# Splitting the streamed weights four chunks ahead in place of three, in a ring of five slots

## The chip, the core and the metric

The kernel runs on one core of one Trainium2 chip. The metric is device time in microseconds (us) of one execution. Engines are called by their names here: TensorE (PE) multiplies, VectorE (DVE) and ScalarE (ACT) do elementwise work, GpSimd (POOL) does some elementwise work and issues transfers, SyncE (SP) issues transfers alone.

## What is computed

Two transformer-like layers run one after the other on x, 256 tokens of width 1024, all in float32:

- First layer: a norm, one projection to queries, keys, values and gates, a differential attention (8 heads) and a chunk attention (8 heads), two branch projections weighed by gates, an output projection; then a norm and a product-key retrieval of experts ("peer"): top-16 of top-16 candidates per head, and for all 16384 experts `hid = gelu(u . x)` times a gate that is zero for those that were not picked, and a sum with the value rows v.
- Second layer: a feed-forward part (`silu(gate) * up`, width 2816), a mixer of a linear recurrence and a sliding-window attention, a second feed-forward part, each with norms before and after.

```
xn   = rmsnorm(h, norm1_w);  proj = xn @ w_in
h    = h + (g_d*(o_d @ w_branch_diff) + g_c*(o_c @ w_branch_chunk)) @ w_out
h    = h + peer(rmsnorm(h, norm2_w), ...)
x    = x + 0.5*rms_norm(swiglu(rms_norm(x)))
x    = x + rms_norm(hybrid_mixer(rms_norm(x)))
x    = x + 0.5*rms_norm(swiglu(rms_norm(x)))
```

## The kernel before

**The stream of weights.** All weights lie in DRAM as 244 chunks of 128 x 2048 float32 (1 MB each) in the order of their use: `qkd` 8, `vd` 4, `vc` 2, `qkc` 4, `gate` 8, `bd` 4, `bc` 2, `out` 4, `wq` 4, `pu` 64 (hidden units of the experts), `pv` 64 (their values), `gu1` 22, `dn1` 11, `in2` 7, `wo` 4, `gu2` 22, `dn2` 11. Every float32 product is made of three matmuls on two parts: for a weight w, `wh` is w rounded to the matmul's short form, and `wl = w - wh`; likewise `xh` and `xl`. `three` (L1917 to L1919) issues high x high, high x low, low x high.

**The ring.** `raw`, `wh` and `wl` have `RING = 5` slots each; chunk c uses slot c % 5. `raw` and `wl` share one memory (L101 to L105): the low part is written over the raw chunk, so a slot can be filled again only when TensorE has finished the chunk in it. Four engines pass a chunk on:

1. SyncE (L401) waits for `c_done`, which TensorE raises at the end of each chunk, and issues the transfer of chunk c+5 into the slot of chunk c. This we call the refill.
2. ScalarE, `split(c)` (L557 to L561): waits for the landing (`raw_in[slot]`) and casts raw to `wh`, one instruction of 128 x 2048.
3. VectorE, `low(c, slot)` (L967 to L970): waits for that cast (`w_high`) and subtracts, one instruction of 128 x 2048 (L969).
4. TensorE waits for `w_low` and runs the chunk: 48 matmuls of 256 columns, or 24 of 512.

```
def ahead(c):
    if c + AHEAD < NCH:
        split(c + AHEAD)
```

**What sets the order.** Each engine has one program, written by hand, and works through it in order. `ahead(c)` stands in the programs of ScalarE and VectorE at the places that belong to TensorE's chunk c, between the other work of that chunk, and splits the chunk `AHEAD` later. `ahead_in(i, c)` (L568, L976) is the same inside the loops over the expert values. Two short runs at the start split the first chunks.

**The stages in which other work stands beside the splits.**

- Attention of the first layer, 24 steps n (two steps to a chunk of `qkc` and `gate`). TensorE's step: transpose the weights of step n (L2042), scores of step n+2 (L2032), one half of a chunk (`gates_beside(n + 1)`, 24 matmuls), values of step n (`output`, L2056). In an even step that half ends a chunk and raises `c_done`. ScalarE's step: scale the output of step n-1 (L691), copy the transposed weights of step n to memory (L682), exponentials of step n+2 (L673), and in even steps `ahead(CH["qkc"] + n // 2 + 1)`. TensorE's values of step n wait for the copy of step n.
- Branch projections `bd`, `bc` (VectorE L1334, L1349 to L1355): VectorE takes each finished unit out of the two banks of `ub`, and TensorE may begin the next but one only then.
- Experts, hidden part (`pu`): TensorE one chunk a step, ScalarE gelu (L766). From hidden step 34 to 57 a step also spreads the gates of one or two groups of 8 tokens (1, 1, 2 in turn): VectorE makes the one-hot rows of a group (L1462, L1467, L1471: `one1`, `one2`, `g2`), TensorE multiplies them (L2161), ScalarE copies them out (L785), and every sixth step GpSimd stores 4 MB of gates (L479). VectorE's step: one-hot rows of step n, then `ahead` of step n.
- Experts, value part (`pv`): ScalarE casts the activations (L804), VectorE subtracts (L1489), GpSimd multiplies by the gate (L499) and issues two loads of 256 KB a chunk.
- Between the parts: the sum of a stage in `acc` is squared on ScalarE (L599), and VectorE computes the norm's root and the diagonal `dg` with which TensorE transposes the next input.

Of the kernel before, what the change touches and what calls it, by code (L numbers as in the profile page):

```python
# [40 lines left out]

CW = 2048
RING = 5
AHEAD = 3
_sizes = [("qkd", 8), ("vd", 4), ("vc", 2), ("qkc", 4), ("gate", 8), ("bd", 4), ("bc", 2), ("out", 4),
          ("wq", 4), ("pu", 64), ("pv", 64), ("gu1", 22), ("dn1", 11), ("in2", 7), ("wo", 4),
          ("gu2", 22), ("dn2", 11)]
# [42 lines left out]
def build_program(nc, A, out):  # L90
    ctx = ExitStack()
    with ctx:
# [463 lines left out]
        def _(act):  # L556
            def split(c):  # L557

                slot = c % RING
                act.wait_ge(raw_in[slot], c // RING * 16 + 16)  # L560
                act.copy(wh[:, slot, :], raw[:, slot, :]).then_inc(w_high, 1)  # L561
# [6 lines that stand above are left out]
            def ahead_in(i, c):  # L568

                c += AHEAD  # L570
                slot = c % RING
# [23 lines left out]
            def square(src, scratch, col, scale=1.0):  # L595

                if nsq[0]:
                    act.wait_ge(sq_ok, nsq[0])
                act.activation(scratch[:, 0:src.shape[1]], src, ACT.Square, scale=scale,  # L599
                               accum_out=ssq[:, col:col + 1]).then_inc(sq_ok, 1)  # L600
                nsq[0] += 1
# [25 lines left out]
            def resid_of(tt):  # L627
                return resid[:, tt, :]
# [19 lines left out]
            split(1)  # L648
            act.wait_ge(x_in[1], 16)
            square(resid_of(1), junk, 1)  # L650
            split(2)

            for j in range(8):
                ahead(j)
# [303 lines left out]
        def _(v):  # L958
# [8 lines left out]
            def low(c, slot):  # L967
                v.wait_ge(w_high, c + 1)
                v.tensor_tensor(wl[:, slot, :], raw[:, slot, :], wh[:, slot, :].bitcast(F32),  # L969
                                ALU.subtract).then_inc(w_low, 1)  # L970

            def ahead(c):
                if c + AHEAD < NCH:
                    low(c + AHEAD, (c + AHEAD) % RING)

            def ahead_in(i, c):  # L976

                low(i * VBODY + (c + AHEAD), (c + AHEAD) % RING)

# [231 lines left out]
                v.wait_ge(c_done, i * 4 + (j + 1))  # L1211
                scaled(qkT[:, bass.ds(i * 8 + 2 * j, 2), :], j % 2 if (i, j) != (0, 2) else None).then_inc(u_free, 1)

            low(AHEAD - 1, AHEAD - 1)
            ahead(0)
            scale_row()
            for j in range(3):
# [1203 lines left out]
```

## Time and profile before

| | |
|---|---|
| median of 3 runs | 1504.12 us (1503.8 to 1507.4) |
| the profiled execution, time | 1504.91 us |
| the profiled execution, span | 1503.4 us |
| TensorE busy | 1484.8 us (99%), weight loads 1372.2 us |
| VectorE busy | 1067.2 us (71%) |
| ScalarE busy | 729.6 us (49%) |
| GpSimd busy | 306.4 us (20%) |
| DMA | 329.76 MB, 219 GB/s over the span |
| mean granted TensorE clock | 0.999 |

The span is what the profile's rows lie in; the device time of the same execution is 1.5 us longer. An engine's share is a mean over stages with different limits; TensorE's 99% is nearly the same in all of them.

### The profile page before, as it was taken

To read this page: it belongs to the slowest core of one execution; us is meant where nothing else is said; L and a number is where in the kernel's file an instruction comes from. 1 tells how busy PE (TensorE), PEld (TensorE's weight loads), DVE (VectorE), ACT (ScalarE), POOL (GpSimd) and SP (SyncE) were. 2 spreads that over 40 slices of the span, in tenths; PEclk is the share of its full clock that TensorE was granted. 3 is DMA by queue.
4 is the path that set the end of the run, shared out by engine and by line. 5 is a ranking of instruction groups with operands and counts; after the bars stand their busy time and mean duration, and the time that the engine had idled before them with its cause. 6 is when DMAs were issued, how large, how long until landed. Compare 5 with 4: busy or idle time off the path is not lost.

```text
span 1503.4 us, 26972 instructions
## 1 busy us (share of the span) xinstructions
PE 1484.8 (99%) x10794; PEld 1372.2 (91%) x10794; DVE 1067.2 (71%) x1583; ACT 729.6 (49%) x853; POOL 306.4 (20%) x306
## 2 busy tenths in 40 slices
PE   8999999999999999999999999999999999999998
PEld 8989998999999999998888888888999898899986
DVE  5667676699999898946555555566877476787753
ACT  5366653544454454544444444445444458644441
POOL 2000000000110111125666677650000010000000
PEclk9999999999999999999999999999999999999999
DMA  8644354576666678888888788775555543455552
GB/s 305 204 157 141 122 172 173 191 245 242 234 226 214 214 253 278 286 304 312 288 288 288 288 292 292 284 272 182 197 197 196 196 162 113 154 170 196 182 187 80
DMA packets 56697, 329.76 MB, mean 219 GB/s; under 512 B 7536, under 2 KB 7584, under 8 KB 25232
## 3 DMA queue, kind: packets, MB, share of 16 engines
q1 hardware_dynamic: 36288, 259.01, 50.4%
q0 software_dynamic: 20304, 69.21, 12.6%
q8 instruction: 82, 1.34, 0.4%
q14 instruction: 23, 0.19, 0.0%
HBM read 294.64 MB, written 33.55 MB: 218 GB/s over the span
## 4 chain that ended last, share of the span: by engine, by line
PE 94%; DVE 3%; ACT 2%; issue 0%; DMA 0%; DVEq 0%; ACTq 0%
PE ub L1917 17%; PE ub L1918 17%; PE ub L1919 17%; PE acc L1919 11%; PE acc L1917 11%; PE acc L1918 11%; PE acc L2161 3%; PE acc L2032 1%; PE mb L2056 1%; PE mb L1919 1%; PE mb L1918 1%; PE mb L1917 1%; DVE wl L969 1%; PE mb L2042 0%; ACT junk_again L599 0%
## 5 line engine op out<-in xcount | busy, mean ns | idle before, releaser
L969 DVE TENSOR_TENSOR wl<-raw,wh 128x2048 fp32r<-128x2048 f32 x244 | 561.1, 2303 | 201.5 <-ACT wh L561 137.3
L1917 PE MATMUL ub<-xh,wh 128*128 128x256 f32 x2168 | 610.9, 282 | 0.8 <-DVE wl L1195 0.8
L1919 PE MATMUL ub<-xh,wl 128*128 128x256 f32 x2168 | 603.2, 278 | 0.0
L1918 PE MATMUL ub<-xl,wh 128*128 128x256 f32 x2168 | 603.2, 278 | 0.0
L1917 PEld LDWEIGHTS ub<-xh,wh 128*128 128x128 f32 x2168 | 408.1, 188 | 8.9 <-issue 6.1
L1918 PEld LDWEIGHTS ub<-xl,wh 128*128 128x128 f32 x2168 | 409.6, 189 | 0.1
L1919 PEld LDWEIGHTS ub<-xh,wl 128*128 128x128 f32 x2168 | 409.4, 189 | 0.0
L561 ACT CAST wh<-raw 128x2048 fp32r<-128x2048 f32 x184 | 350.6, 1907 | 118.6 <-DMA raw<-in_wstream 118.5
L1917 PE MATMUL acc<-wh,ah 128*128 128x512 f32 x512 | 199.4, 389 | 1.1 <-issue 1.1
L1919 PE MATMUL acc<-wh,al 128*128 128x512 f32 x512 | 199.2, 389 | 0.0
L1918 PE MATMUL acc<-wl,ah 128*128 128x512 f32 x512 | 199.2, 389 | 0.0
L499 POOL TENSOR_TENSOR hid<-hid,gl_in 128x512 f32<-128x512 f32 x64 | 157.9, 2469 | 16.7 <-DMA gl_in<-gates 15.8
L804 ACT CAST ah<-hid 128x512 fp32r<-128x512 f32 x64 | 39.9, 623 | 187.6 <-PE acc L1919 185.2
L766 ACT ACTIVATE hid<-ub 128x512 f32<-128x512 f32 x64 | 38.3, 599 | 159.5 <-PE ub L1919 158.3
L1917 PEld LDWEIGHTS acc<-wh,ah 128*128 128x128 f32 x512 | 96.1, 188 | 21.0 <-issue 1.3
L573 ACT CAST wh<-raw 128x2048 fp32r<-128x2048 f32 x60 | 114.2, 1904 | 0.8 <-DMA raw<-in_wstream 0.8
L1919 PEld LDWEIGHTS acc<-wh,al 128*128 128x128 f32 x512 | 96.1, 188 | 20.0
L1918 PEld LDWEIGHTS acc<-wl,ah 128*128 128x128 f32 x512 | 96.1, 188 | 20.0
L462 POOL DMA_DIRECT2D hidden<-hid x60 | 32.6, 544 | 366.9 <-ACT hid L766 366.9
L1489 DVE TENSOR_TENSOR al<-hid,ah 128x512 fp32r<-128x512 f32 x64 | 49.2, 768 | 81.8 <-ACT ah L804 81.8
L842 ACT ACTIVATE fs<-fg 128x256 f32<-128x256 f32 x44 | 18.4, 418 | 137.5 <-DVE fg L1085 137.5
L1919 PE MATMUL acc<-wh,fl 128*128 128x512 f32 x176 | 68.5, 389 | 0.0
(379 smaller groups left out, 1759.2 us busy)
## 6 DMA issues: line engine op xcount, KB each, us to landing
raw<-in_wstream SPq DMA_DIRECT2D x244, 1024.0 KB, 4.9
gates<-gst POOLq DMA_DIRECT2D x16, 1024.0 KB, 14.7
gl_in<-gates POOLq DMA_DIRECT2D x64, 256.0 KB, 3.7
hidden<-hid POOLq DMA_DIRECT2D x60, 256.0 KB, 4.9
hid<-hidden POOLq DMA_DIRECT2D x60, 256.0 KB, 3.6
resid<-in_x SPq DMA_DIRECT2D x2, 512.0 KB, 4.2
rb<-in_rel POOLq DMA_DIRECT2D x1, 1024.0 KB, 6.0
wb<-in_ffn_post_g POOLq DMA_DIRECT2D x2, 512.0 KB, 4.8
```

Of the source, the lines that this page charges most:

```text
L462: pool.dma_start(hidden[bass.ds(n + 4, 1)].rearrange("a p n -> p (a n)"), hid[:, k, :, :].rearrange("p a b -> p (a b)")).then_inc(spill[k] ...
L499: pool.tensor_tensor(h, h, gl_in[:, k, :].rearrange("p (g j t) -> p j g t", g=TG, j=2), ALU.mult).then_inc(hd_m, 1)
L561: act.copy(wh[:, slot, :], raw[:, slot, :]).then_inc(w_high, 1)
L573: act.copy(wh[:, slot, :], raw[:, slot, :]).then_inc(w_high, 1)
L766: act.activation(hid[:, nmod % 4, :, :].rearrange("p a b -> p (a b)"), ub[:, nmod % 2, :], ACT.Gelu).then_inc(hd_g, 1)
L804: act.copy(ah[:, nmod % 2, :, :], hid[:, nmod % 4, :, :]).then_inc(a_h, 1)
L969: v.tensor_tensor(wl[:, slot, :], raw[:, slot, :], wh[:, slot, :].bitcast(F32), ALU.subtract).then_inc(w_low, 1)
L1489: v.tensor_tensor(al[:, k % 2, :, :], hid[:, k % 4, :, :], ah[:, k % 2, :, :].bitcast(F32), ALU.subtract).then_inc(a_l, 1)
L1917: pe.matmul(dst, sh, mh, start=first, stop=False)
L1918: pe.matmul(dst, sh, ml, start=False, stop=False)
L1919: return pe.matmul(dst, sl, mh, start=False, stop=last)
L2161: last = pe.matmul(dst, g2[:, b, part, :, k], one2[:, b, k, :], start=part == 0, stop=part == 2)
```

## The change

`AHEAD` becomes 4, and the two runs at the start split one chunk more. Nothing else is changed: ring, transfers, TensorE's program and what is computed stay as they are.

```diff
 CW = 2048
 RING = 5
-AHEAD = 3
+AHEAD = RING - 1
...
             square(resid_of(1), junk, 1)
-            split(2)
+            for c in range(2, AHEAD):
+                split(c)
...
-            low(AHEAD - 1, AHEAD - 1)
+            for c in range(2, AHEAD):
+                low(c, c)
             ahead(0)
             scale_row()
```

What this does to the order. The orders of TensorE, GpSimd and SyncE are the same before and after. On VectorE the first difference is at the start, between the diagonal `dg` of the first norm and the copy `rt` of its row. Before:

```order
L1066 TENSOR_SCALAR dg<-ident,rstd 128x128
L969 TENSOR_TENSOR wl<-raw,wh 128x2048 [waits w_high] x2
L1080 COPY rt<-mb 128x256 [waits sc_ps]
L1085 TENSOR_TENSOR qkT<-ub,rt 128x512 [waits c_done,dve]
L1085 TENSOR_TENSOR qkT<-ub,rt 128x512 [waits c_done]
```

and with the change:

```order
L1067 TENSOR_SCALAR dg<-ident,rstd 128x128
L970 TENSOR_TENSOR wl<-raw,wh 128x2048 [waits w_high] x3
L1081 COPY rt<-mb 128x256 [waits sc_ps]
L1086 TENSOR_TENSOR qkT<-ub,rt 128x512 [waits c_done,dve]
L1086 TENSOR_TENSOR qkT<-ub,rt 128x512 [waits c_done]
```

One subtraction more stands ahead of the copy; from there to the last chunks each subtraction of a chunk stands where that of the chunk before it stood.

On ScalarE the kinds of instructions stand in the same order afterwards, but each cast waits for another slot. The opening and step 0 of the first attention (`p_sb` exponentials, `pT` the transposed weights, `y` the output), before:

```order
L561 CAST wh<-raw 128x2048 [waits raw_in2]
L682 COPY pT<-mb 128x128 [waits at_t]
L673 ACTIVATE p_sb,rs<-s_sb,smx 128x128 [waits at_b]
L673 ACTIVATE p_sb,rs<-s_sb,smx 128x128
L561 CAST wh<-raw 128x2048 [waits raw_in3]
L691 ACTIVATE y<-mb,rr 128x128 [waits at_o]
L682 COPY pT<-mb 128x256 [waits at_t]
```

and with the change:

```order
L561 CAST wh<-raw 128x2048 [waits raw_in3]
L683 COPY pT<-mb 128x128 [waits at_t]
L674 ACTIVATE p_sb,rs<-s_sb,smx 128x128 [waits at_b]
L674 ACTIVATE p_sb,rs<-s_sb,smx 128x128
L561 CAST wh<-raw 128x2048 [waits raw_in4]
L692 ACTIVATE y<-mb,rr 128x128 [waits at_o]
L683 COPY pT<-mb 128x256 [waits at_t]
```

The cast of step 0 moved from slot 3 to slot 4. Chunk `qkc` + 0, number 14, is in slot 4, and TensorE finishes it in the same step 0.

The first steps of the gates' part of the experts on ScalarE (`hid` gelu, `gst` the copied gates), before:

```order
L779 CAST gT<-mb 128x128
L561 CAST wh<-raw 128x2048 [waits raw_in2]
L766 ACTIVATE hid<-ub 128x512 [waits spill2,c_done]
L785 COPY gst<-acc 128x128x8 [waits g_ps]
L561 CAST wh<-raw 128x2048 [waits raw_in3]
```

and with the change:

```order
L780 CAST gT<-mb 128x128
L561 CAST wh<-raw 128x2048 [waits raw_in3]
L767 ACTIVATE hid<-ub 128x512 [waits spill2,c_done]
L786 COPY gst<-acc 128x128x8 [waits g_ps]
L561 CAST wh<-raw 128x2048 [waits raw_in4]
```

Again each cast waits for the slot that was filled one chunk later than the slot it waited for before.

## Rows read from the trace of the kernel before

**Rows 1.** The page, busy time and share of TensorE and its weight loads.

```profile
PE 1484.8 (99%) x10794; PEld 1372.2 (91%) x10794; DVE 1067.2 (71%) x1583; ACT 729.6 (49%) x853; POOL 306.4 (20%) x306
```

**Rows 2.** Waits of TensorE: us in total, times, longest.

```profile
PE mb L1823 <- DMA resid<-in_x: 4.8, 1, 4.8
...
PE acc L1917 <- DVE wl L969: 1.2, 1, 1.2
```

**Rows 3.** Timeline of SyncE's queue at 96 us: start, us, engine, line.

```profile
96.29 0.33 SPq L401 DMA_DIRECT2D raw<-in_wstream  x1
```

**Rows 4.** Landing of refills: at 96, 516 to 534, 538 to 555, 700 to 1020.

```profile
DMA to landing us min/median/max: 4.9/4.9/4.9
...
DMA to landing us min/median/max: 8.9/10.5/10.9
...
DMA to landing us min/median/max: 5.2/5.2/6.6
...
DMA to landing us min/median/max: 4.7/4.9/5.8
```

**Rows 5.** Timeline of ScalarE, attention steps 0 and 1.

```profile
94.66 1.89 ACT L561 CAST wh<-raw 128x2048 fp32r<-128x2048 f32 x1
96.46 0.36 ACT L691 ACTIVATE y<-mb,rr 128x128 f32<-128x128 f32 x1
96.72 0.35 ACT L682 COPY pT<-mb 128x256 f32<-128x256 f32 x1
```

**Rows 6.** Timeline of TensorE, values of attention steps 0, 1 and 2.

```profile
95.95 0.38 PE L2056 MATMUL mb<-vd,pT 128*128 128x128 f32 x2
...
99.96 0.61 PE L2056 MATMUL mb<-vd,pT 128*128 128x128 f32 x4
...
103.87 0.38 PE L2056 MATMUL mb<-vd,pT 128*128 128x128 f32 x2
```

**Rows 7.** Timeline of ScalarE, gates' part: gelu of two steps.

```profile
540.59 0.60 ACT L766 ACTIVATE hid<-ub 128x512 f32<-128x512 f32 x1 [2.68 <-PE ub L1919]
...
547.64 0.60 ACT L766 ACTIVATE hid<-ub 128x512 f32<-128x512 f32 x1 [2.68 <-PE ub L1919]
```

**Rows 8.** Timeline of VectorE, gates' part: first one-hot instruction of two groups.

```profile
547.21 0.68 DVE L1462 TENSOR_TENSOR one<-iota,i1T 128x1024 bf16<-128x1024 bf16 x1
...
550.72 0.69 DVE L1462 TENSOR_TENSOR one<-iota,i1T 128x1024 bf16<-128x1024 bf16 x1
```

**Rows 9.** Timeline of VectorE at places between the parts.

```profile
213.64 2.29 DVE L969 TENSOR_TENSOR wl<-raw,wh 128x2048 fp32r<-128x2048 f32 x1 [1.08 <-ACT wh L561]
215.85 0.68 DVE L1349 TENSOR_TENSOR gate<-ub,gate 128x512 f32<-128x512 f32 x1
...
239.23 1.22 DVE L1172 TENSOR_TENSOR resid<-resid,acc 128x1024 f32<-128x1024 f32 x1 [1.83 <-PE acc L1919]
...
1210.34 1.22 DVE L1113 TENSOR_TENSOR y_again<-acc,wb 128x1024 f32<-128x1024 f32 x1 [2.83 <-ACT junk_again L599]
```

**Rows 10.** Timeline of ScalarE at places between the parts.

```profile
217.99 1.91 ACT L561 CAST wh<-raw 128x2048 fp32r<-128x2048 f32 x1 [4.38 <-DMA raw<-in_wstream]
...
664.97 1.91 ACT L561 CAST wh<-raw 128x2048 fp32r<-128x2048 f32 x1 [4.87 <-DMA raw<-in_wstream]
...
1286.39 1.06 ACT L931 ACTIVATE gl<-gl 128x1024 f32<-128x1024 f32 x1
```

**Rows 11.** Timeline of ScalarE, value part: cast of the activations, two chunks.

```profile
764.26 0.62 ACT L804 CAST ah<-hid 128x512 fp32r<-128x512 f32 x1 [3.01 <-PE acc L1919]
...
769.71 0.62 ACT L804 CAST ah<-hid 128x512 fp32r<-128x512 f32 x1 [3.01 <-PE acc L1919]
```

**Rows 12.** Timeline of VectorE, value part: low part of the activations.

```profile
764.92 0.69 DVE L1489 TENSOR_TENSOR al<-hid,ah 128x512 fp32r<-128x512 f32 x1 [1.34 <-ACT ah L804]
```

**Rows 13.** Timeline of TensorE: a matmul at 9.8 us, one at 18 us.

```profile
9.80 0.41 PE L1919 MATMUL ub<-xh,wl 128*128 128x256 f32 x1
...
18.04 0.28 PE L1918 MATMUL ub<-xl,wh 128*128 128x256 f32 x1
```

## The prediction
> **What bounds the kernel now.** I read the page's busy times first: TensorE is busy 1484.8 us of 1503.4 [rows 1]. Then the waits of TensorE: the longest is 4.8 us, for x at the very start, and for the split weights (`wl`) it waits 1.2 us, once [rows 2]. So TensorE sets the time throughout, and an earlier split has next to nothing to give back: even if every wait for weights went, that is 1.2 us. The question is therefore what the change can do to TensorE's cover. For that I read the queue of SyncE with the landings, and then the timelines of ScalarE, TensorE and VectorE in each stage.
>
> **What the change really moves.** The ring decides when a chunk can be split, not `AHEAD`: chunk m can land only after TensorE has ended chunk m-5. With `AHEAD` 3 the step of chunk c asks for c+3, whose refill was issued at the end of c-2; with 4 it asks for c+4, issued at the end of c-1. The transfer starts no earlier than before; what comes earlier is the place of the waiting cast in ScalarE's program, and of the waiting subtraction in VectorE's. Everything behind them in those in-order programs now waits for a refill issued one chunk later. The price of one turn of the ring: the refill of the chunk that ended at 96.1 is issued at 96.29 [rows 3] and lands 4.9 us later [rows 4]; the cast takes 1.9 [rows 5], the subtraction 2.3 [rows 9]. So, after the end of a chunk, the cast is done at +7.0 and the subtraction at +9.3. Where a stage needs something that stands behind them sooner than that, TensorE stalls. No instruction, byte or matmul is added.
>
> **Attention of the first layer, the largest term.** In even steps TensorE ends a chunk in the half that stands before `output(n)`. ScalarE's cast of the same step now asks for the slot of just that chunk. Before, the cast of step 0 began at 94.66 without a wait, and then came the output scaling at 96.46 and the copy `pT` of step 1 at 96.72, ended at 97.07 [rows 5]; TensorE used that copy at 99.96 [rows 6]. Now the cast begins at 96.29 + 4.9 = 101.2 and the copy follows it by as much as before: it ends at 101.2 + (97.07 - 94.66) = 103.6. TensorE's values of step 1 begin there and not at 99.96: a stall of 3.65 us. Nothing recovers it, since the next chunk ends a fixed piece of TensorE's work after that point, and its refill starts the same wait again: the two-step period goes from 103.87 - 95.95 = 7.9 us [rows 6] to 11.6. There are 11 such even steps (n = 0 to 20): 11 x 3.65 = 40 us. In the last steps outputs and copies are a little longer, but so is TensorE's step; I leave 3.65. Bounds: 3.4 and 4.0 a step, 37 to 44 us.
>
> **The gates' part of the experts, the second term.** Here VectorE makes the one-hot rows of step n+1 behind the subtraction of step n. One group takes 550.72 - 547.21 = 3.5 us [rows 8]. From the issue of a refill the first group is ready after landing + 1.9 + 2.3 + 3.5 = landing + 7.7, and the second of a step 3.5 later. TensorE wants the first two steps after the chunk's end: 2 x (547.64 - 540.59) = 14.1 us [rows 7], and the second 1.6 us later (the time of one spread, a step of 7.05 less a chunk of 5.44). With a landing of 5.2 [rows 4] the first is ready at 12.9: no stall; but the second comes at 16.4 against 15.7 at the most, so steps with two groups lose about 1 to 2 us. While GpSimd's stores of the gates run, a refill lands after 8.9 to 10.9 [rows 4]; then the first group is ready at 18.6 against 14.1, a stall of 4.5 us, and the two refills behind it find the room that this stall made. Step by step through the 24 steps: 4.2 us at the entry (the one-hots stand behind the cast of chunk 37, which the last top-k steps did not need to wait for), 8 steps of two groups at 1 to 1.9, and three of the four stores at 4.7. The sum is 4.2 + 8 x 1.5 + 3 x 4.7 = 30 us. Bounds: 11 us if landings stay at 5.2 throughout (the stalled kernel has fewer refills to a store), 35 if each store costs a little more.
>
> **Places between the parts.** The same wait, met once each. Branch projections: VectorE's gating of the first `bc` unit began at 215.85, behind a subtraction from 213.64 [rows 9]. It now stands behind the subtraction of the next chunk, cast from 217.99 to 219.9 [rows 10] and subtracted until 222.2: 6.4 us later, of which 0.9 was slack, so 5.5. Output projection to `wq`: the add to the residual at 239.23 [rows 9] moves behind a subtraction that ends at 243.0, and 2.7 us of it reach the diagonal that TensorE waits for. End of the hidden part: the cast at 664.97 waited 4.9 us for its landing [rows 10]; the gelu that stands behind it now is one that TensorE needs at 664.95, so 2.5. `dn1` to `in2`: the norm at 1210.34 [rows 9] is held back 3.2 by the subtraction of the chunk whose refill is issued at 1203.8, and ScalarE's cast ahead of the next norm adds 0.4: 3.6. `wo`: the gelu at 1286.39 [rows 10] moves 2.8 back, behind a cast that must wait until 1286, and the cast ahead of the norm of the second feed-forward part adds 1.4: 4.2. Entries of the first attention and of the first feed-forward part, an estimate from the same +9.3: 3.4. Together 5.5 + 2.7 + 2.5 + 3.6 + 4.2 + 3.4 = 22. Bounds 12 and 28.
>
> **The value part.** After the end of a chunk the cast is done at +7.0, the subtraction at +9.3, and the low part of the activations (0.7, [rows 12]) at +10.0. TensorE wants it after two chunks, 2 x (769.71 - 764.26) = 10.9 [rows 11]. So 0.9 us are left a chunk, and with landings of 4.7 to 5.8 [rows 4] it just holds. But GpSimd's two loads move with the low part and will start together with the refill. I take 4 us for the first chunks, where landings are longer; the bounds are 0 and 26 (a landing that grows by 1.8 makes each of 60 chunks 0.43 longer).
>
> **Where it costs nothing.** Projections at the start, `wq`, the top-k steps (VectorE is behind there: each subtraction begins after its cast would be done also now), the bodies of both feed-forward parts, and the end (fewer splits are left): the work that hides it is TensorE's own 5.4 us chunk, since only a copy needed two chunks later stands behind the cast. In several of these stretches ScalarE already waits for landings, as at 217.99 [rows 10], and nothing moves.
>
> **The sum.** 40 + 30 + 22 + 4 = 96 us. The profiled execution took 1504.9, 0.8 above the median of 1504.1; on the median's footing I predict 1600 us.
>
> **Rivals.** (1) *The stalls also slow the matmuls.* After TensorE's idle start its matmuls of 256 columns are shown 0.41 us long, later 0.28 [rows 13], although the granted clock reads 1.00 in both stretches, so the rows do not tell this pace as the clock. If it came back after each attention stall, the 3.9 us of TensorE's work between a stall and the next end of a chunk would take up to twice that: up to 11 x 3.9 = 43 us more, about 1640. Against it: no row shows the pace fall after the short gaps of this kernel, but none of them is as long as 3.65. The Trainium skill, TensorE: Matmul & The Clock Gate, section "Why this matters for your kernels", says that idle gaps between bursts of matmuls can put TensorE back to its lower clock; by that rule the sum would be this rival's, and without it 1600. (2) *The value part stalls throughout:* the landing grows by the full 1.8 us because two loads stand in front of each refill: 1600 + 22 = 1622. For it speaks the small slack of 0.9, against it that the refills of that part landed within 5.8. (3) *Only the attention pays:* the gates' landings shorten and the places between find slack: 1504 + 40 + 11 + 12 = 1567. (4) *Not slower:* the wait changes hands. If ScalarE reached the cast of an even attention step after the refill had landed, the deeper split would hide there, TensorE's 1.2 us for `wl` would go, and the time would be 1503. It decides whether the landing (issue + 4.9) comes before ScalarE is at the cast (94.66 to 96.5); the rows put it at 101.2, so this needs ScalarE to be 5 us late, and nothing makes it so.
>
> **How the numbers follow.** Forecast 0.68, rival 1 0.12, rival 2 0.10, rival 3 0.08, rival 4 0.02. The forecast's own bounds are 37 + 11 + 12 + 0 = 60 and 44 + 35 + 28 + 26 = 133 us, that is 1564 to 1637; ends of all terms on one side at once are unlikely. I set 1570 to 1640, which takes in rivals 2 and most of 1, and leaves out about 2 in 10. A difference of 0.3% is 4.5 us, about what can be told from no change here. All cases but rival 4 are far slower: slower 0.98, same 0.015, faster 0.005.
>
> **What would show it.** TensorE's row of waits should gain two long entries: values (L2056) waiting for the copy of `pT` (L682), 11 times about 3.7 us, and spreads (L2161) waiting for the one-hot product (L1471), about a dozen times, 30 us. ScalarE's waits for landings (L561) should grow most in the attention, and the distance between refills there should be 11.6 us. The bodies of the feed-forward parts should keep 5.44 us a chunk. I am wrong if the attention's refills stay 7.9 us apart, or if the granted clock falls below 1.00 there.

## The result and the profile after

The changed kernel takes 1642.88 us (median of 4 runs, 1639.78 to 1648.12) against 1504.13: a ratio of 1.0926, 95% interval 1.0902 to 1.0949. It is slower by 139 us where 96 were forecast, and lies 3 us above the end of the range. The profiled execution has a span of 1642.7 us, 139.3 more than before.

The page of the changed kernel, busy time and the granted clock in 40 slices of 41 us (before: [rows 1], and a clock of 1.00 nearly throughout):

```profile
PE 1534.1 (93%) x10794; PEld 1400.9 (85%) x10794; DVE 1109.9 (68%) x1583; ACT 728.1 (44%) x853; POOL 263.9 (16%) x306
...
PEclk9988889999999999989999999999999999999999
```

TensorE runs the same 10794 matmuls and is busy 49.3 us longer (1534.1 against 1484.8). So about 90 of the 139 us are idle time, as the forecast had it. The rest is shown as busy: matmuls that ran slower, which the forecast had left out of its sum, and in the value part stalls too short for these rows.

Waits of TensorE in the changed kernel (before: [rows 2]; line numbers above 651 are one or two higher than before, so L2058 is the old L2056 and L2163 the old L2161):

```profile
PE mb L2058 <- ACT pT L683: 38.6, 11, 3.7
PE acc L2163 <- DVE g L1473: 23.5, 11, 4.6
PE acc L1919 <- DVE al L1491: 8.7, 19, 1.9
...
PE mb L1851 <- DVE dg L1108: 4.1, 2, 2.6
PE ub L1919 <- DVE gate L1351: 3.1, 1, 3.1
PE ub L1919 <- ACT hid L767: 2.6, 1, 2.6
PE mb L2044 <- DVE p_sb L1273: 2.3, 1, 2.3
```

The first row is the forecast's main term nearly to the digit: 11 waits of 3.5 us in the mean. The second is the gates' part with its entry, the third the value part, and the four short rows are places between the parts. In the value part the waits of the weight loads have to be read too (7.2 us for `wl`, 5.9 for `al`): TensorE is shown busy for 359.3 us there against 349.1 before, at a granted clock of 1.00 in both, so the rows of the matmuls count such short stalls as busy.

ScalarE in step 1 of the first attention, and then TensorE around the wait that it causes (before: [rows 5, 6]):

```profile
104.73 1.90 ACT L561 CAST wh<-raw 128x2048 fp32r<-128x2048 f32 x1 [7.40 <-DMA raw<-in_wstream]
106.53 0.36 ACT L692 ACTIVATE y<-mb,rr 128x128 f32<-128x128 f32 x1
106.79 0.36 ACT L683 COPY pT<-mb 128x256 f32<-128x256 f32 x1
```

```profile
103.61 0.28 PE L1921 MATMUL ub<-xh,wl 128*128 128x256 f32 x1
107.21 1.23 PE L2058 MATMUL mb<-vd,pT 128*128 128x128 f32 x4 [3.32 <-ACT pT L683]
...
109.69 0.41 PE L1920 MATMUL ub<-xl,wh 128*128 128x256 f32 x1
109.90 0.41 PE L1921 MATMUL ub<-xh,wl 128*128 128x256 f32 x1
...
113.31 0.29 PE L1919 MATMUL ub<-xh,wh 128*128 128x256 f32 x1
113.44 0.28 PE L1920 MATMUL ub<-xl,wh 128*128 128x256 f32 x1
```

ScalarE waits 7.4 us for a landing and only then makes the 0.36 us copy that TensorE needs. Behind the 3.3 us gap TensorE's matmuls of 256 columns start 0.21 us apart, until 6 us after its end, and then 0.12 apart again: the two levels, 1.2 and 2.4 GHz. The refills of the attention, 7.9 us apart before, now come 13.1 to 15.8 us apart; the forecast had 11.6. It had also named its sign of being wrong, a granted clock below 1.00 in the attention, and this came true. The stretches of the changed kernel show the clock (the columns: stretch, its length, busy time and instructions of PE, PEld, DVE, ACT and POOL, granted clock, DMA share, GB/s); they are the 6 us behind that gap, the first attention, the branch and output projections, the gates' part and the value part. Under them stands the attention before:

```profile
107.20:113.30 6.10, 6.09 (x27) 5.54 (x28) 3.64 (x9) 2.34 (x10) 0.00 (x0) 0.50 0.00 0
...
88.40:257.00 168.60, 127.71 (x833) 114.85 (x832) 75.28 (x238) 68.00 (x181) 5.09 (x6) 0.83 0.24 79
257.00:322.90 65.90, 57.97 (x395) 53.31 (x393) 38.58 (x46) 27.18 (x24) 1.63 (x2) 0.97 0.44 148
553.00:761.00 208.00, 187.60 (x1873) 184.79 (x1873) 159.90 (x118) 86.78 (x77) 26.39 (x35) 0.94 0.62 209
798.00:1168.00 370.00, 359.33 (x1542) 287.22 (x1543) 242.30 (x132) 156.05 (x131) 179.45 (x182) 1.00 0.75 267
```

```profile
88.80:188.70 99.90, 99.90 (x833) 90.92 (x833) 72.34 (x237) 67.94 (x180) 5.10 (x6) 1.00 0.40 134
```

The attention is 68.7 us longer for the same 833 matmuls: 40.9 us are idle, and the busy time grew by 27.8. Divided at the same instructions in both traces, the 139.3 us fall like this:

| part | before | after | more | forecast |
|---|---|---|---|---|
| first attention | 99.9 | 168.6 | 68.7 | 40 |
| gates' part, with its entry | 373.3 | 407.8 | 34.5 | 30 |
| value part | 349.1 | 369.5 | 20.4 | 4 |
| everything else | | | 15.7 | 22 |

(The entry of the gates' part is counted from the key scores on, 196.7 us before and 200.0 after, and the spreads themselves take 176.6 and 207.8. The row of the first attention holds that part's entry, about 3 us, which the forecast had among its 22. The last row is 20.5 us at the other places between the parts, less 4 us by which the chunks of `gu2` went through faster and 1 us in small differences; the last section comes back to these 4.)

### The profile page after: what moved, and what is told of

It reads as the page before. It is cut to its first block, busy times and chain, and to the rows that moved or that the text cites. A ratio compares the mean times of both kernels' runs of the same rounds, so it can differ in the third digit from the quotient of the medians.

```text
span 1642.7 us, 26972 instructions
## 1 busy us (share of the span) xinstructions
PE 1534.1 (93%) x10794; PEld 1400.9 (85%) x10794; DVE 1109.9 (68%) x1583; ACT 728.1 (44%) x853; POOL 263.9 (16%) x306
## 4 chain that ended last, share of the span: by engine, by line
PE 66%; DMA 16%; DVE 7%; ACT 5%; issue 5%; SPq 0%; DVEq 0%
DMA raw<-in_wstream 16%; PE ub L1919 14%; PE ub L1921 13%; PE ub L1920 13%; PE acc L1919 7%; PE acc L1921 7%; PE acc L1920 7%; ACT wh L561 2%; ACT wh L573 2%; DVE wl L970 2%; DVE g L1473 2%; PE acc L2163 1%; DVE one L1469 1%; PE mb L2058 1%; DVE al L1491 1%
## 5 line engine op out<-in xcount | busy, mean ns | idle before, releaser
L970 DVE TENSOR_TENSOR wl<-raw,wh 128x2048 fp32r<-128x2048 f32 x244 | 588.3, 2412 | 383.9 <-ACT wh L561 263.3
L1919 PE MATMUL ub<-xh,wh 128*128 128x256 f32 x2168 | 620.1, 286 | 5.2 <-ACT hid L767 2.6
L1919 PEld LDWEIGHTS ub<-xh,wh 128*128 128x128 f32 x2168 | 417.4, 193 | 15.2 <-issue 8.4
L1920 PEld LDWEIGHTS ub<-xl,wh 128*128 128x128 f32 x2168 | 419.1, 193 | 0.1
L1921 PEld LDWEIGHTS ub<-xh,wl 128*128 128x128 f32 x2168 | 417.2, 192 | 0.0
L499 POOL TENSOR_TENSOR hid<-hid,gl_in 128x512 f32<-128x512 f32 x64 | 117.2, 1833 | 9.8 <-DMA gl_in<-gates 8.9
L2163 PE MATMUL acc<-one,g 128*128 128x128 bf16 x768 | 60.2, 242 | 23.6 <-DVE g L1473 23.5
L2163 PEld LDWEIGHTS acc<-one,g 128*128 128x128 bf16 x768 | 55.4, 150 | 26.6 <-DVE g L1473 25.8
L1491 DVE TENSOR_TENSOR al<-hid,ah 128x512 fp32r<-128x512 f32 x64 | 69.5, 1086 | 0.6 <-ACT ah L805 0.6
L1920 PE MATMUL acc<-wl,fh 128*128 128x512 f32 x176 | 68.5, 389 | 0.0
```

What stands on the lines that cost most here:

```text
L499: pool.tensor_tensor(h, h, gl_in[:, k, :].rearrange("p (g j t) -> p j g t", g=TG, j=2), ALU.mult).then_inc(hd_m, 1)
L1491: v.tensor_tensor(al[:, k % 2, :, :], hid[:, k % 4, :, :], ah[:, k % 2, :, :].bitcast(F32), ALU.subtract).then_inc(a_l, 1)
L1919: pe.matmul(dst, sh, mh, start=first, stop=False)
L1920: pe.matmul(dst, sh, ml, start=False, stop=False)
L1921: return pe.matmul(dst, sl, mh, start=False, stop=last)
L2163: last = pe.matmul(dst, g2[:, b, part, :, k], one2[:, b, k, :], start=part == 0, stop=part == 2)
```

## The experiments

All kernels take their distance from a function of the step's chunk in place of the constant, in the programs of ScalarE and VectorE alike, so that each part can have its own. A step whose distance is one more than that of the step before splits two chunks, one whose distance is one less splits none:

```diff
-                if c + AHEAD < NCH:
-                    split(c + AHEAD)
+                while nsplit[0] < min(NCH, c + distance(c) + 1):
+                    split(nsplit[0])
+                    nsplit[0] += 1
```

Each ratio below is to the kernel before, measured beside it on the same chip; in us it is the ratio times 1504.

### Each part alone

**attn4**: `distance` returns 4 for `CH["qkc"] <= c < CH["bd"]`, else 3.

> Distance four only in the steps of the first attention, three in all the others. In the changed kernel that part took 168.6 us against 99.9 (from the first scores to the first matmul of the branch projections). If the parts are independent, this kernel takes 1504 + 69 = 1573 us, with 11 waits of 3.7 us for the copy of pT and a granted clock near 0.83 in that stretch. If instead part of the 69 us comes from chunks that arrived late from the part before (which here still splits three ahead), it takes 1560 or less.

Measured 1572.01 us, ratio 1.0421 (1.0403 to 1.0439), +63 us; TensorE waits 11 times for the copy of `pT`, 38.7 us, and the stretch is 165.7 us long. The part is independent of the others. (The 3 us less than in the changed kernel are the entry, where this kernel still splits three ahead.)

**gates4**: 4 for hidden steps 34 to 57, else 3.

> Distance four only in hidden steps 34 to 57, which spread the gates. That part took 207.8 us against 176.6 in the changed kernel, and its entry about 3 more. If the parts are independent: 1504 + 31 to 34 = 1535 to 1538 us, with about 11 waits for the one-hot product, 23 us together. If the entry or the late refills of the neighbours carry part of it, it is 1520 to 1530.

Measured 1538.83 us, ratio 1.0202 (1.0185 to 1.0219), +30 us. TensorE waits 13 times for the one-hot product, 21.7 us together, and the part grew from 176.6 to 209.4 us.

**value4**: 4 for the value part, else 3.

> Distance four only in the value part of the experts (64 chunks). That part took 370.0 us in the changed kernel against 349.6 (first to last matmul of acc<-wh,ah). If the parts are independent: 20 us more than before. VectorE's subtraction should take 2.3 to 3.8 us in place of 2.3, and its low part of the activations up to 1.8 in place of 0.7, in about half of the chunks.

Measured 1525.38 us, ratio 1.0143 (1.0115 to 1.0171), +22 us, and the part takes 370.3 us.

**rest4**: 3 in those three parts, 4 everywhere else.

> Distance four everywhere except in the first attention, the gates' part and the value part, which keep three. If the parts are independent: 139 us of the whole change less 66 (attention), 33 (gates) and 20 (value part) is 20 us, total about 1524. The prediction had 22 for these places. If the stalls of the parts feed each other across their borders, it is 1510 or less.

Measured 1529.08 us, ratio 1.0173 (1.0135 to 1.0211), +26 us. Its waits of over 1.6 us, without the one for x at the start:

```profile
PE mb L1863 <- DVE dg L1118: 4.2, 2, 2.8
PE acc L2175 <- DVE g L1483: 3.5, 1, 3.5
PE ub L1931 <- DVE gate L1361: 3.3, 1, 3.3
PE ub L1931 <- ACT hid L774: 2.5, 1, 2.5
PE mb L2056 <- DVE p_sb L1283: 2.2, 1, 2.2
PE mb L1837 <- DVE resid L1127: 2.0, 1, 2.0
PE mb L1888 <- DVE dg L1118: 1.8, 3, 1.2
PE acc L2334 <- DVE gr L1758: 1.7, 1, 1.7
```

These are the forecast's places, one by one: `dg` behind the output projection, entry of the gates' part, `bc`, end of the hidden part, entry of the attention, `dn1` to `in2`, and the two at `wo`. (Of the 4.2 us for `dg`, 1.6 were there before the change. The entry of the gates' part, 3.5 us, the forecast had counted with that part and not among these places.) The four ratios add up to 63 + 30 + 22 + 26 = 141 us, with about 8 either way by their intervals, and the whole change costs 139: within that, the parts do not feed each other.

### Place or distance

**attn4_late**: as attn4, with cast and subtraction one attention step later.

```diff
-                if n % 2 == 0 and n < 22:
+                if n % 2 == 1 and n < 23:
                     ahead(CH["qkc"] + n // 2 + 1)
...
-                if n % 2 == 1 and n < 22:
-                    ahead(CH["qkc"] + (n + 1) // 2)
+                if n % 2 == 0 and 2 <= n < 23:
+                    ahead(CH["qkc"] + n // 2)
```

> As the run before, but cast and subtraction stand one attention step later in the programs of ScalarE and VectorE (odd steps), so that the copies of the next step stand ahead of the waiting cast. Theory, it is the place in the queue that costs: the cast is then done at about issue + 7.0, and the copy that TensorE wants 7.8 us after the chunk's end is made in time; attention loses 0 to 15 us, total 1504 to 1519. Rival, it is the distance itself (the refill issued a chunk later): the attention keeps its period of 14 us and the total stays near 1573.

Measured 1512.26 us, ratio 1.0050 (1.0030 to 1.0071), +7.5 us in place of 63. No wait for `pT` is left. ScalarE's queue now reads:

```profile
100.81 1.91 ACT L565 CAST wh<-raw 128x2048 fp32r<-128x2048 f32 x1 [0.17 <-DMA raw<-in_wstream]
102.63 0.35 ACT L697 ACTIVATE y<-mb,rr 128x128 f32<-128x128 f32 x1
102.88 0.25 ACT L688 COPY pT<-mb 128x128 f32<-128x128 f32 x1
```

The same cast of the same refill waits 0.17 us here, since the two copies that TensorE needs first stand ahead of it. What is left are short waits for VectorE, most of them for a unit taken out of `ub` (7 of about 0.55 us), whose subtraction is now in front of that. The cost lies in what stands behind the waiting cast; that the chunk was refilled one chunk later costs next to nothing. But nothing is gained either.

### The clock

**attn4_filled**: as attn4, with matmuls in TensorE's gap; their result is not used.

```diff
                 def output(n):
                     b = n % 2
+                    if n0 == 0 and n % 2 == 1 and n < 22:
+                        for _ in range(28):
+                            pe.matmul(acc[:, 0, 256:512], xh[:, 1, 0:P], xh[:, 0, :], start=True, stop=True)
                     pe.wait_ge(at_v, n0 + n + 1)
```

> As attn4, with 28 more matmuls of 256 columns (3.2 us, their result is not used) put ahead of TensorE's wait in each odd step of the first attention, so that the engine has no gap longer than 0.5 us. Theory, idle gaps bring the granted clock down, and that is 28 of the 69 us: the clock stays at 1.00, the two-step period is 11.6 us in place of 14.6, and the total is 1504 + 40 = 1544. Rival, the slow matmuls have another cause than the gaps: the clock stays near 0.83 and the total is 1573 or more, since the added matmuls are slow as well.

Measured 1551.41 us, ratio 1.0281 (1.0258 to 1.0305), +42 us. The first attention of attn4, and then of attn4_filled:

```profile
88.30:254.00 165.70, 126.98 (x833) 114.29 (x832) 75.23 (x238) 68.48 (x181) 5.09 (x6) 0.84 0.24 81
```

```profile
88.30:232.00 143.70, 140.45 (x1141) 128.90 (x1140) 74.23 (x237) 68.14 (x181) 5.09 (x6) 1.00 0.28 94
```

With 308 matmuls more (x1141) the part is 22 us shorter, and the clock stands at 1.00. The gaps bring the clock down; without them the part costs 43.8 us more than before. That is the price of the stalls alone, 4.0 us for each of the 11 in place of the forecast's 3.65: the refills come 11.5 to 12.8 us apart, one of them landing after 6.0 us in place of 4.9. The filling itself adds nothing to it, as in each of the 11 steps it ends before the copy of `pT` is done, or within 0.1 us of it. The Trainium skill, TensorE: Matmul & The Clock Gate, section "Why this matters for your kernels", says that idle gaps between bursts of matmuls put TensorE back to its lower clock, and by that rule the sum was rival 1's. The trace agrees with the rule: 0.84 with the gaps and 1.00 without them.

### The value part: two causes that stand in for each other

GpSimd's multiply and VectorE in value4. GpSimd, then VectorE:

```profile
864.18 1.30 POOL L503 TENSOR_TENSOR hid<-hid,gl_in 128x512 f32<-128x512 f32 x1
...
870.24 2.29 POOL L503 TENSOR_TENSOR hid<-hid,gl_in 128x512 f32<-128x512 f32 x1
```

```profile
864.22 3.42 DVE L977 TENSOR_TENSOR wl<-raw,wh 128x2048 fp32r<-128x2048 f32 x1 [1.90 <-ACT wh L578]
867.57 0.68 DVE L1499 TENSOR_TENSOR al<-hid,ah 128x512 fp32r<-128x512 f32 x1
869.08 2.29 DVE L977 TENSOR_TENSOR wl<-raw,wh 128x2048 fp32r<-128x2048 f32 x1 [0.84 <-ACT wh L578]
871.29 1.78 DVE L1499 TENSOR_TENSOR al<-hid,ah 128x512 fp32r<-128x512 f32 x1
```

Where GpSimd's multiply starts first (864.18), VectorE's subtraction takes 3.42 us in place of 2.29. Where the subtraction runs first (869.08), the multiply takes 2.29 in place of 1.30 and ends at 872.53, and VectorE's low part waits in its turn: 1.78 in place of 0.69. In the whole part of value4, 28 of 65 subtractions and 25 of 64 low parts are longer than the 2.29 and 0.69 us that they take alone (before: 2 of 64 and 6 of 64). Before the change the multiply was the slow one (2.7 us in 45 of 63 chunks), and TensorE did not wait for it. The Trainium skill, SBUF — State Buffer, section "SBUF: two separate sides", says that an instruction of VectorE that reads two inputs from SBUF, as both of these do, and one of GpSimd take turns at one pair of ports, each for its whole length. These rows agree to within 0.2 us.

**value4_nomult**: `pool.tensor_tensor` on `h[:, 0:1, 0:1, 0:8]` alone.

> As value4, but GpSimd multiplies 8 of 512 columns of the hidden units by their gates and leaves the rest as it is; loads are the same. Theory, the 20 us come from GpSimd's multiply (1.3 us) running beside VectorE's two instructions, which then last longer by 0.9 us a chunk in the mean: without it they keep 2.3 and 0.7, the 0.9 us of slack a chunk is back, and the kernel loses 0 to 5 us to the one before. Rival, the refill lands later because two loads start beside it: 20 us are lost as in value4.

**value4_smallload**: both loads of a chunk bring `[:, 0:32]` (that of the gates from chunk 4 on).

> As value4, with the multiply, but the two loads of a chunk (hidden units and gates) bring 32 of 512 columns each from chunk 4 on. Theory (GpSimd's multiply): little changes, VectorE's instructions are still long in half of the chunks and 12 to 20 us are lost. Rival (the loads delay the refill): landings fall to about 4.0 us and the loss falls to 0 to 5 us.

**value4_neither**: both cuts.

> As value4, with both cuts of the last two runs together: GpSimd multiplies 8 of 512 columns and its loads bring 32 of 512. Theory, two causes that stand in for each other (the multiply beside VectorE's instructions, and the loads beside the refill; where one is gone the other grows): with neither, the chain end of chunk to low part of the activations takes the predicted 10.0 us of 10.9, and 0 to 4 us are lost to the kernel before. Rival, the chain itself is too long by 0.3 us a chunk whatever GpSimd does: about 20 us are lost again.

| kernel | us | ratio | part, us |
|---|---|---|---|
| value4 | 1525.38 | 1.0143 (1.0115 to 1.0171) | 370.3 |
| value4_nomult | 1522.49 | 1.0134 (1.0107 to 1.0161) | 372.7 |
| value4_smallload | 1523.78 | 1.0128 (1.0103 to 1.0153) | 367.7 |
| value4_neither | 1510.89 | 1.0034 (1.0011 to 1.0056) | 356.2 |

Both theories of a single cause missed: each cut alone left the loss where it was. Landing of the refill (KB, us) and VectorE's low part (count, busy time, mean ns, idle before) from 690 to 1030 us, in nomult, in smallload and in neither:

```profile
raw<-in_wstream SPq DMA_DIRECT2D x59, 1024.0 KB, 5.4
...
L1500 DVE TENSOR_TENSOR al<-hid,ah 128x512 fp32r<-128x512 f32 x59 | 40.5, 686 | 1.8 <-ACT ah L811 1.8
```

```profile
raw<-in_wstream SPq DMA_DIRECT2D x59, 1024.0 KB, 4.9
...
L1502 DVE TENSOR_TENSOR al<-hid,ah 128x512 fp32r<-128x512 f32 x60 | 73.7, 1229 | 0.0
```

```profile
raw<-in_wstream SPq DMA_DIRECT2D x61, 1024.0 KB, 4.9
...
L1503 DVE TENSOR_TENSOR al<-hid,ah 128x512 fp32r<-128x512 f32 x62 | 42.4, 684 | 0.0
```

Without the multiply VectorE keeps its 0.69 us, but refills land later: 5.4 in the middle, and 14 of 55 over 6 us (in value4 2 of 56). Why they land later then, no run shows. Without the loads every refill but one lands within 6 us, but the multiply meets VectorE more often: 1.23 us in the mean. Only with neither is the part down to 7 us more than before, three waits (5.2 us together), two of them behind single landings of 7.3 and 7.5. From the issue of a refill to the end of the low part it now takes 9.7 us in the middle, and 10.9 in value4. So the chain that the forecast worked out (10.0 us of 10.9) holds when nothing disturbs it, and either disturbance alone eats the 0.9 us.

### The gates' part

**gates4_smallstore**: as gates4; each store writes a sixteenth (`n = slice(16 * c, 16 * c + 1)`), and the value part loads other data for gates.

> As gates4, but each store of gates writes a sixteenth of its 4 MB (the value part reads other data in their place). Theory of the prediction: the late refills beside the stores cause the stalls of over 4 us (and with them most of the low clock); without them a refill lands after 5.2, only steps with two groups lose up to 1 us, and of the 33 us that gates4 lost in this part 5 to 15 are left. Rival, the one-hot rows behind the subtraction are too late whatever the stores do: 25 us or more are left.

Measured 1513.76 us, ratio 1.0060 (1.0038 to 1.0082), +9 us in place of 30. TensorE's waits for the one-hot product, in gates4 and then here:

```profile
PE acc L2173 <- DVE g L1481: 21.7, 13, 4.4
```

```profile
PE acc L2176 <- DVE g L1484: 8.4, 10, 1.7
```

The part takes 189.0 us in place of 209.4, and its refills land after 5.3 us in the middle in place of 6.1. The long waits go with the stores. Ten short ones are left, 8.4 us, and seven of them, with 7.5 us, stand in the steps with two groups. TensorE's busy time in the part goes from 187.6 us to 180.7 (177.8 before) and its granted clock from 0.94 to 0.99, so the low clock came with the long waits as well.

### The other direction, and the end of the kernel

**ahead2**: 2 everywhere.

> Distance two everywhere. The refill that a cast asks for is then one chunk older than before, so ScalarE's waits for landings go to nearly nothing; what is at stake is the margin of TensorE: the subtraction ends one chunk closer to its use. In the parts with the cast at the step's start 5.4 us of margin are left after 2.3 + 1.9, so theory: within 10 us of before, any loss sitting where VectorE is behind (the top-k steps). Rival: the margin is gone in many parts and TensorE waits for wl, 30 us or more.

Measured 1576.54 us, ratio 1.0479 (1.0441 to 1.0518), +72 us. My expectation missed, and its rival holds:

```profile
PE ub L1929 <- DVE wl L977: 41.7, 16, 5.2
```

The loss lies in the first chunks (the start takes 97.7 us in place of 88.8) and in the two feed-forward parts (26 and 27 us more). There TensorE waits some 3 us for `wl` again and again, and at 1085 to 1095 us the clock is 0.83. Three is the best of the three distances.

**ends4**: 4 from `gu2` on, else 3.

> Distance four only from gu2 on (the last 33 chunks). In the changed kernel this stretch took 194.8 us against 197.7, as the chunks of gu2 came 5.4 us apart in place of 5.65. If that gain belongs to the distance, this kernel is 2 to 4 us faster than before (0.2%); if it is an accident of what the stretch before left, no difference.

Measured 1505.63 us, ratio 1.0008 (0.9992 to 1.0024): no difference. The 3 us that the changed kernel seemed to win there are not the distance's (see the last section). None of these kernels is faster than the kernel before.

## Why the prediction was off

The mechanism, its places and its sign were right; the sum was 43 us short. Two steps failed: the sum put at nothing what the stalls do to TensorE's clock, and it took the value part at 4 us. The runs showed 22 us for the clock in the attention and about 10 in the gates' part, and 20 for the value part. That rival 1's own number, about 1640, lies so near the 1643 measured is luck: the clock cost less than its 43 us, and the value part made up for it.

- **Attention, 40 us:** the waits measured 38.6, and the part with the gaps filled 43.8 more, within the bounds of 37 to 44. Right. What failed is that the sum stopped at "Nothing recovers it": nothing did, and more was lost. The matmuls were busy 27.8 us longer, and 22 us of that are net loss, as the filled kernel shows. This was rival 1, which I priced at up to 43 and gave 0.12, because no row showed the clock fall after a short gap. No gap between bursts in that trace was as long as 3.65 us, so the rows did not speak against it at all. One pair of rows even spoke for it: the matmuls of [rows 13] at 9.8 us are 0.41 us long and 0.21 apart, as those at the granted clock of 0.50 in the changed kernel, so after TensorE's idle start that trace too shows the pace of the lower level, although the view prints 1.00 there. The clock belonged in the sum.
- **Gates' part, 30 us:** 34.5, and 30 by itself, without the entry. Idle and clock share it differently than I had it: about 23.5 us of waits and 10 of slower matmuls. The entry took 3.5 us where I said 4.2. Three waits of 4.0 to 4.6 us came with the stores, as forecast; seven short ones in the steps with two groups make 7 us together, where I had 8 of 1.5.
- **Places between the parts, 22 us:** right. rest4 measured 26 (20 to 32) together with the entry of the gates' part, for which the forecast had 22 + 4.2; in the whole change these places take 20.5 us and the attention's entry about 3. The 15.7 of the table are less only because `gu2` ran 4 us faster. The waits at `bc` took 4.7 of 5.5 (1.4 and 3.3), `dg` 2.6 of 2.7, the end of the hidden part 2.5 of 2.5.
- **Value part, 4 us:** 20.4. This is the term that was mis-sized. I saw the slack of 0.9 us and that the two loads would start together with the refill, and took the lower end. I did not look at what GpSimd's multiply would then meet. Rival 2 named 22 us with a wrong mechanism: the landing stayed at 4.9 us in the middle in value4.
- **"Costs nothing" in projections, top-k and the feed-forward bodies:** right; the top-k steps and `wq` moved by under 0.3 us apart from the entry, and the chunks of `gu1` stayed at 5.44 us.

With the clock (28 in the attention, 10 in the gates' part) and 20 for the value part, the same working gives 40 + 30 + 22 + 4 + 28 + 10 + 16 = 150, against 139 measured. Of the 11 us too much, 5.5 lie in the gates' part, mostly its short waits, and 4 are the faster `gu2`; the rest is small differences in the other rows.

## What to carry to other kernels

With a ring, the depth of the ring sets how early data can arrive, and the look-ahead only sets where an in-order engine stops to wait for it: for each waiting instruction ask what stands behind it and who needs that, and put the short copies that the busiest engine wants ahead of it (63 us became 7.5 here by two conditions). In attn4 38.7 us of waits in a dense stream of matmuls came with a loss of 65.8 us, so price the clock together with the gap. Where a slack of a few tenths of a us is left, take the loss, not the zero: several small disturbances can each use it up, and removing one of them shows nothing.

## What was not expected of the hardware

- In ahead2 gaps of 2.98 us were enough for a granted clock of 0.83; after the gap that ends at 1100.43 matmuls ran 0.12 us apart for 1.1 us, then 0.21 apart for 3.3 us. In attn4_late, gaps of 0.6 us left the clock at 1.00. The length of a gap alone does not tell: in gates4 the clock was 0.50 from 513.9 to 517.3 us, behind a gap of 1.78, and in rest4 it stayed at 1.00 behind one of 3.30 that ended at 226.7.
- The steady chunks of `gu1` came 5.44 us apart in the profiles of before and value4 and 5.65 in those of attn4 and ends4, although program and data are the same there, which moves the part by 3.8 us (183.0 and 186.8). The chunks of `gu2` do the same: 5.65 us in the profiles of before and value4, 5.44 in those of the changed kernel, rest4 and also value4_nomult, whose distance there is still three. So these 4 us are not the distance's. No run here explains them. They are nearly as large as the 4.5 us under which the prediction saw no change.
- The waits of GpSimd and VectorE for each other change sides with the order in which they start: 2.7 us multiplies and 2.29 us subtractions in most chunks before the change, 1.3 us multiplies in most chunks and subtractions of up to 4.6 us after it.
